# The last pair's results go to their tokens by products with a weight matrix, and the table of the other results is read and added beside them

## The reference, cut to what matters

```python
x = first_block(...)             # mixing part, then: x = x + hier_moe(rms_norm(x), ...)
h = x
h = h + mixers(rmsnorm(h)) ...   # second layer
h = h + hier_moe_2(rmsnorm(h), ...)
return rmsnorm(h, norm_final)

# either MoE, for token t with experts e1, e2 and gates g1, g2:
#   y_e(t) = (silu(x_t @ w1[e]) * (x_t @ w3[e])) @ w2[e]
#   h_t    = h_t + g1 * y_e1(t) + g2 * y_e2(t)
```

## Time and profile before

| | us |
|---|---|
| median of 3 runs (lowest, highest) | 2476.98 (2476.9, 2477.67) |
| the profiled execution's own time | 2479.46 |
| its span in the trace | 2477.7 |
| PE busy | 2146.9 (87%) |
| DVE busy | 694.2 (28%) |
| ACT busy | 351.8 (14%) |
| POOL busy | 124.4 (5%) |

### The profile page before, as it was taken

How to read it: one execution, slowest core, us unless ns; L and a number is a source line. 1 busy time by engine, 2 the same in 40 slices (tenths; PEclk the granted TensorE clock), 3 DMA queues, 4 the chain that set the end, 5 groups by cost and what they waited for, 6 DMA issues and landing times.

```text
span 2477.7 us, 26940 instructions
## 1 busy us (share of the span) xinstructions
PE 2146.9 (87%) x11637; PEld 1061.0 (43%) x11637; DVE 694.2 (28%) x1734; ACT 351.8 (14%) x675; POOL 124.4 (5%) x154
## 2 busy tenths in 40 slices
PE   7999999969878787399999999999999697787883
PEld 3455444434333333155665754445554343333331
DVE  2236561241000000213678554121022410000002
ACT  3101220110000000012222442100021100000001
POOL 4000000000000000001011100000000000000000
PEclk9999999979999989789999999999999699999996
DMA  5212112449999999721100101152332499999994
GB/s 192 92 35 88 49 42 95 178 176 422 427 427 428 426 427 428 257 85 26 28 3 2 70 1 59 61 203 97 107 136 85 148 427 427 426 428 427 426 428 178
DMA packets 92714, 524.29 MB, mean 212 GB/s; under 512 B 13013, under 2 KB 27530, under 8 KB 66986
## 3 DMA queue, kind: packets, MB, share of 16 engines
q1 hardware_dynamic: 77712, 483.43, 48.1%
q10 hardware_dynamic: 5130, 21.56, 2.3%
q0 software_dynamic: 9744, 17.47, 2.0%
HBM read 514.02 MB, written 25.17 MB: 218 GB/s over the span
## 4 chain that ended last, share of the span: by engine, by line
PE 67%; DMA 23%; DVE 6%; issue 2%; ACT 1%; ACTq 0%; DVEq 0%; POOLq 0%
PE ps L198 64%; DMA SC<-in_w 5%; DMA SC<-in_w_e_up 4%; DMA RING<-in_w_e_up 3%; DMA RING<-in_w 3%; DMA XT<-in_w_e_down 3%; DMA XT<-in_w 3%; DMA SC<-in_w_e_down 1%; DVE X L1680 1%; DMA SC<-ytab 1%; PE ps L363 1%; PE ps L1339 1%; PE ps L2629 0%; DMA ytab<-SC,ST 0%; DMA SC<-xrows,ST 0%
## 5 line engine op out<-in xcount | busy, mean ns | idle before, releaser
L198 PE MATMUL ps<-SC 64*64 64x64 f32 (+4 forms) x5872 | 700.0, 328 | 93.2 <-issue 23.5
L198 PE MATMUL ps<-RING,SC 128*64 128x512 f32 (+2 forms) x1872 | 681.3, 621 | 77.3 <-issue 48.0
L198 PE MATMUL ps<-XT,RING 128*128 128x512 f32 x1104 | 495.2, 602 | 6.1 <-DVE SC L1960 3.3
L198 PEld LDWEIGHTS ps<-SC 64*64 64x64 f32 (+2 forms) x5872 | 341.1, 146 | 329.1 <-issue 291.7
L198 PEld LDWEIGHTS ps<-RING,SC 128*64 128x64 f32 (+2 forms) x1872 | 239.6, 159 | 379.9 <-issue 379.9
L198 PEld LDWEIGHTS ps<-XT,RING 128*128 128x128 f32 x1104 | 208.3, 192 | 255.4 <-issue 248.4
L1474 DVE TENSOR_TENSOR SC<-SC,ps 128x512 f32<-128x512 f32 x32 | 22.0, 688 | 721.8 <-PE ps L198 721.8
L198 PE MATMUL ps<-XT,SC 128*64 128x512 f32 x352 | 161.4, 613 | 21.6 <-DMA SC<-in_w_e_up 10.9
L198 PE MATMUL ps<-RING,XT 128*128 128x512 f32 (+2 forms) x448 | 158.2, 506 | 0.0
L198 PE MATMUL ps<-SC,RING 128*128 128x512 f32 (+2 forms) x448 | 116.2, 426 | 0.0
L198 PEld LDWEIGHTS ps<-RING,XT 128*128 128x128 f32 x448 | 78.0, 201 | 73.6 <-issue 73.2
(11 more groups left out here) (390 smaller groups left out, 1429.1 us busy)
## 6 DMA issues: line engine op xcount, KB each, us to landing
RING<-in_w SPq DMA_DIRECT2D x43, 2048.0 KB, 33.8
SC<-in_w SPq DMA_DIRECT2D x42, 2048.0 KB, 34.1
RING<-in_w_e_gate SPq DMA_DIRECT2D x22, 2048.0 KB, 34.2
SC<-in_w_e_down SPq DMA_DIRECT2D x17, 2048.0 KB, 33.2
RING<-in_w_in SPq DMA_DIRECT2D x16, 2048.0 KB, 8.3
SC<-in_w_e_up SPq DMA_DIRECT2D x16, 2048.0 KB, 34.7
XT<-in_w SPq DMA_DIRECT2D x11, 2048.0 KB, 33.2
RING<-in_w_e_up SPq DMA_DIRECT2D x10, 2048.0 KB, 32.6
```

Of the source, the lines that this page charges most:

```text
L198: return e.matmul(out, l, r, start=st, stop=sp, skip_group_check=True)
```

## The change

In short, and in the order of the code: `ytab` is filled with zeros at the start of the kernel; three masked copies of the gates are made, `gp` for results in rows of pairs before the last, `gh` for the last pair (`LAST` = 15), `go` for overflow pairs; a 128 x 512 matrix `hot` with the gate of the last pair's rows for each token is made on DVE before the last pair's up eviction and turned on PE into `hot2` (rows of the pair by tokens); the last pair isn't scattered: eight products `hot2` (128 tokens of `tt`) times YS (512 columns) give what it adds, and DVE adds these to X out of PSUM; the reads of the table are issued by SP, ahead of `mix2_first` in `moe0`, and DVE adds the table with `gp`, three tiles of it before the first addition of the products. The norm `n2` squares all four tiles on ACT. The final norm multiplies by the gain first and by the root last, shared between DVE and ACT; the gain is loaded by SP.

```diff
     def norm_a(e, m):
-        for i in range(0, m.nt, 2):
+        for i in range(0, m.nt, m.by):                  # n2 has by=1: all four on ACT, none on DVE
...
     def set_g(e):                                       # at its end
+        W.wait_ge(*HG.on("f", 1))
+        e.memset(SC[:, 9, :], 0.0).then_inc(*S.up("g"))
+        W.wait_ge(*S.last("g"))
+        for i in range(4):
+            e.dma_start(ytab.rearrange("(p a b) n -> a p (b n)", a=4, b=2)[i], SC[:, 9, :]).then_inc(*S.up("dz", "zeros"))
...
     def df_a(e):                                        # and likewise in df_v_
+                    if n == "k":
+                        W.wait_ge(*S.on("zeros"))
...
     def s(e):                                           # in moe, after the 96 loads
-            if ahead is not None:
-                ahead(e)
+            for i in (5, 6):
+                for f in slots.put(i, ("yb", bi, i), (c, ("X", NT - 1)))[1]:
+                    W.wait_ge(*f)
+            for x in range(2):
+                W.wait_ge(*slots.on((f"m{bi}", LAST, 2, x)))
+                W.wait_ge(*c.on("y", LAST - 1 - x))
+            for tt in range(NT):
+                e.dma_start(YB[tt], ytv[tt]).then_inc(*c.up(f"dyb{tt}", "yb", tt))
+            ahead(e)
...
     def p(e):                                           # in moe
                 up_p(e, c, q, c.take, w)
                 if q + 1 < NPAIR:
                     turn_e(e, c, q + 1, c.take)
+                else:
+                    b, free = c.take("hot")
+                    W.wait_ge(*free)
+                    W.wait_ge(*c.on("hot"))
+                    for tt in range(NT):
+                        i = e.transpose(b[:, tt * 128:(tt + 1) * 128], hot[:, tt * 128:(tt + 1) * 128], ident[:, :])
+                    i.then_inc(*c.up("p", "hot T"))
                 down_p(e, c, q, c.take, w)
+            for tt in range(NT):
+                for hf in range(2):
+                    b, free = c.take("add", tt, hf)
+                    W.wait_ge(*free)
+                    W.wait_ge(*c.on("ev", "hot"))
+                    W.wait_ge(*c.on("ev", "down", LAST, hf))
+                    mm(e, b[:, :], hot2[:, tt * 128:(tt + 1) * 128], YS[:, LAST % 2, hf * 512:(hf + 1) * 512]).then_inc(*c.up("p", "add", tt, hf))
...
     def a(e):                                           # in moe; ACT evicts hot2 and, for the last pair, both halves of down
+                if q == LAST:
+                    W.wait_ge(*c.on("hot T"))
+                    e.activation(hot2, c.at("hot")[:, :], AF.Copy).then_inc(*c.up("a", "ev", "hot"))
...
-            W.wait_ge(*c.on("y", NPAIR - 1))
-            W.wait_ge(*c.on("y", NPAIR - 2))
-            for tt in range(NT):
-                e.dma_start(YB[tt], ytab.rearrange("(t p c) n -> t p (c n)", p=128, c=2)[tt]).then_inc(*c.up(f"dyb{tt}", "yb", tt))
...
     def v(e):                                           # in moe
+            hots_v(e)
+            up_v(e, c, LAST, c.at)
+            n_over = over(e)
+            for kind, tt in (("table", 0), ("table", 1), ("table", 2), ("add", 0), ("table", 3), ("add", 1), ("add", 2), ("add", 3)):
+                if kind == "table":
+                    W.wait_ge(*c.on("yb", tt))
+                    rows(e, tt, gp, c, "v")
+                else:
+                    for hf in range(2):
+                        xs = X[:, tt, hf * 512:(hf + 1) * 512]
+                        W.wait_ge(*c.on("add", tt, hf))
+                        W.wait_ge(*c.last("v"))
+                        e.tensor_tensor(xs, xs, c.at("add", tt, hf)[:, :], A.add).then_inc(*c.up("v", "ev", "add", tt, hf))
+                    c.also("v", "X", tt)
...
+            segments(e, n_over, pair_v, late)            # the branch now stands behind the additions
...
+        def rows(e, tt, g, f, s):
+            for k in range(2):
+                W.wait_ge(*f.last(s))
+                e.scalar_tensor_tensor(X[:, tt, :], YB[tt][:, k * D:(k + 1) * D], g[:, k, tt:tt + 1], X[:, tt, :], A.mult, A.add).then_inc(*f.up(s))
+        def hots_v(e):
+            W.wait_ge(*c.on("turn", LAST - 1, 1))
+            W.wait_ge(*c.last("v"))
+            for k, dst in ((0, hot), (1, hot2)):
+                for tt in range(NT):
+                    e.tensor_scalar(dst[:, tt * 128:(tt + 1) * 128], iotf[:, :], prf[:, k, tt:tt + 1], gh[:, k, tt:tt + 1], A.is_equal, A.mult).then_inc(*c.up("v"))
+            W.wait_ge(*c.last("v"))
+            e.tensor_tensor(hot, hot, hot2, A.add).then_inc(*c.up("v", "hot"))
...
     def g(e):                                           # in moe
-            scatter(e, c, NPAIR - 1, 0)
...
+    def fn_first(e):                                    # on SP, behind moe1's reads of the table
+        for f in slots.put(4, "fn", (FN, ("y", NT - 1)))[1]:
+            W.wait_ge(*f)
+        e.dma_start(fn_g, t["norm_final_2"].rearrange("(a n) -> a n", a=1).to_broadcast([128, D])).then_inc(*FN.up("dg", "g"))
...
     def fn_v(e):
+        W.wait_ge(*FN.on("g"))
+        for i in range(NT):
+            W.wait_ge(*M1.on("X", i))
+            e.tensor_tensor(fn_Y[:, i, :], X[:, i, :], fn_g, A.mult).then_inc(*FN.up("v", "xg", i))
         W.wait_ge(*FN.on("sq", NT - 1))
         mean_rsq_v(e, FN, fn_R, "nrm", fn_ss, 1.0 / D, 1e-6)
-            e.scalar_tensor_tensor(fn_Y[:, i, :], X[:, i, :], fn_R.y[:, i:i + 1], fn_g, A.mult, A.mult).then_inc(*FN.up("v", "y", i))
+        W.wait_ge(*FN.on("nrm", "rs"))
+        for i in (1, 3):                                # ACT does 0 and 2 in fn_a
+            W.wait_ge(*FN.on("xg", i))
+            e.tensor_scalar(fn_Y[:, i, :], fn_Y[:, i, :], fn_R.y[:, i:i + 1], None, A.mult).then_inc(*FN.up("v", "y", i))
```

More of the change, by code:

```diff
@@ L344, in norm_v @@
         c = m.c
-        for i in range(1, m.nt, 2):
+        for i in range(1, m.nt, 2) if m.by == 2 else ():
             for f, step in m.ready(i):
@@ L348, in norm_v @@
             e.tensor_tensor_reduce(m.xn[:, i, :], m.src[:, i, :], m.src[:, i, :], 1.0, 0.0, A.mult, A.add, m.ss[:, i:i + 1]).then_inc(*c.up("v", "sq", i))
-        for i in range(0, m.nt, 2):
+        for i in range(0, m.nt, m.by):
             W.wait_ge(*c.on("sq", i))
@@ L1243, in moe @@
         OH = st(2 * NT * 32).rearrange("p (k a b) -> p k a b", k=2, b=32)
-        v1, v2, g1, g2 = st(NT), st(NT), st(NT), st(NT)
+        v1, v2 = st(NT), st(NT)
+        G, gp, gh, go = (st(2 * NT).rearrange("p (a b) -> p a b", a=2) for _ in range(4))
+        g1, g2 = G[:, 0, :], G[:, 1, :]
         hots = [(st(NT * n).rearrange("p (a b) -> p a b", b=n), st(NT)) for n in (4, 8, 8)]
@@ L1265, in moe @@
         NPAIR = NE // 2
+        LAST = NPAIR - 1
+        hot, hot2 = XG[:, LAST % 2 ^ 1, 0:512], XG[:, LAST % 2 ^ 1, 512:1024]
+        ytv = ytab.rearrange("(t p c) n -> t p (c n)", p=128, c=2)
         RT = Flow(book, f"rt{bi}", (3, 4, 5, 6, 7))
@@ L1282, in s @@
                 slots.put(n, f"free{n}", *users)
-            slots.put(6, "free6", *((RT, ("xrows", tt)) for tt in range(NT)))
+            slots.put(6, "free6", (RT, ("xrows",)))
             for p in range(NPAIR):
@@ L1304, in load, with over, segments @@
                         e.dma_start(view(slots.views[4 + n % 3], j), WS[j][bass.ds(i_, 1)].rearrange("a (p k) n -> p (a k) n", p=128)).then_inc(*o.up(f"dw{n % 3}", "load", q, j, x))
-            segments(e, load)
+            segments(e, over(e), load)
             join(e)
-        def segments(e, body):
+        def over(e):
             W.wait_ge(*c.on("nov"))
-            v = e.value_load(nov[0:1, NOV:NOV + 1], min_val=0, max_val=NOV)
+            return e.value_load(nov[0:1, NOV:NOV + 1], min_val=0, max_val=NOV)
+        def segments(e, v, body, after=None):
             def one(q):
@@ L1321, in one @@
                         one(q + 1)
+                    if q == 0 and after is not None:
+                        after()
                     e.wait_ge(*c.on("nov"))
@@ L1413, in pair_p @@
                 down_p(e, o, q, banks, ow)
-            segments(e, pair_p)
+            segments(e, over(e), pair_p)
             join(e)
@@ L1672, in pair_v, with late @@
                 down_v(e, o, q, fixed_at)
-            segments(e, pair_v)
-            join(e)
-            for tt in range(NT):
-                W.wait_ge(*c.on("yb", tt))
-                for k, gk in ((0, g1), (1, g2)):
-                    W.wait_ge(*c.last("v"))
-                    e.scalar_tensor_tensor(X[:, tt, :], YB[tt][:, k * D:(k + 1) * D], gk[:, tt:tt + 1], X[:, tt, :], A.mult, A.add).then_inc(*c.up("v"))
-                c.also("v", "X", tt)
+            def late():
+                e.wait_ge(*o.on("yb"))
+                for tt in range(NT):
+                    rows(e, tt, go, o, "x")
+                o.also("x", "X")
+            segments(e, n_over, pair_v, late)
+            join(e)
+        def rows(e, tt, g, f, s):
[6 more added lines that the diff above has]
+            for k, dst in ((0, hot), (1, hot2)):
```

(12 more changed lines are left out.)

46 lines of the change are left out of this document (26 added, 20 removed).

## The result

The changed kernel took 2463.99 us (median of 4 runs, 2458.94 to 2464.41) against 2477.32 for the kernel before beside it (4 runs, 2476.90 to 2479.44). The ratio is 0.994, with a 95% interval of 0.9923 to 0.9957, so it is faster by 13.3 us. The forecast was 2463.6. The profiled execution went from 2479.46 to 2464.04 and its span from 2477.7 to 2462.3, 15.4 us less.

The account below looks back on a forecast made before the run. Each MoE was taken as bound by its weight loads, which the change leaves alone; only serial end pieces of 39 and 36 us could be won. -14.5 + 1.1 = -13.4 us, median 2476.98 to 2463.6, range 2460 to 2468.

Parts of the forecast that it names:

- When the reads start: Table reads issue at 1012.1 in the first MoE, 16 us earlier; at 2441.85 in the second, held by slot 5.
- DVE's run: Table and product additions on DVE at both MoE ends take 16.6 us, against 10.7 before, with no wait inside.
- The four reads come in faster than this: At both ends, table reads land faster than DVE's 1.34 us per operation, so DVE sets the pace.
- A DVE wait on a product: Sign against the forecast: DVE waiting for PE's products; these were expected in time, lateness taken as 0.
- The first end: End of the first MoE: earlier reads, less the longer DVE run, gain 14.5 us, bounds 11.5 to 15.5.
- From there on the work is as before: After the root starts at 1034.9 in the first end's norm, nothing changes, so the first lx product comes at 1044.9.
- The cover of the loads: mix2 loads move behind the table reads; wl lands at 1033 with 12 us of cover, so cost 0.
- The rival that it comes late: After the first MoE, wl completes at 1048.3, 3.4 us after PE wants it: 2467.0 us; chance 9%.
- The second end: End of the second MoE and final norm: loss 1.1 us, bounds -0.5 to 2.5; last tile 1.65 us later.
- The branch: On DVE between the second end's last addition and the gain products: costs 0.4 us, at most 1.8.
- The zeros: Table zeros written from about 40 us end by 52, cost 0; rival that they delay k's eviction: 2525, chance 4%.
- both ends gain: Rival: without slot 5 as last wait, second-end reads start at 2432.0, DVE ends 9.9 us earlier: 2453.7; chance 4%.

Follow-up runs that it names:

- the kernel with slot 2: Changed kernel, but in the second MoE the table's upper half is read into slot 2 instead of slot 5: 2453.52 us, ratio 0.991.
- the kernels that have one end each: Changed kernel with the old path put back in the other MoE and its norm: first end alone 2460.40 us, second end alone 2478.26 us.
- the kernel with the first end alone: Changed kernel with the second MoE and final norm put back as before: 2460.40 us, ratio 0.9935.
- the second trace of the changed kernel: The changed kernel run once more with no edit: 2461.58 us, ratio 0.994 to the kernel before.
- the kernel with the loads first: Changed kernel, but in the first MoE SP issues the next layer's 11 loads ahead of the table reads: 2483.31 us, ratio 1.0027.

## Why the prediction was right

**When the reads start: right at both ends.** Predicted 1012.1, measured 1012.47, by the landing of the last down weights (1012.31), as the kernel without that wait shows: there they go out at 1002.22. They were to go out about 1 us before the last down products begin; the reads went out 2.4 to 2.6 us before them in five traces and 0.1 us behind their start in three, since those products follow PE's work before them and not the reads. At the second end they go out at 2424.68, the moment in which ACT begins to evict the last down products. That the slot, not the reads' other conditions, holds them there was the central step, and the kernel with slot 2 shows it.

**DVE's run: the way right, its length short.** Predicted 16.6 us, with 16 to 17 and no wait inside as the sign. At the first end it was 17.1 (1017.37 to 1034.44), at the second 17.9 (2429.53 to 2447.44), of which 0.95 is a wait for the second read, and there the sign failed. "The four reads come in faster than this" did not hold: the second read landed 8.0 us after its issue (2425.05), 0.95 us after DVE wanted it. What the prediction left out is the load of the final gain, which SP issues 0.65 us behind the last read (2426.65). Where that load follows the reads, the second read took 7.6 to 8.4 us, in all eleven such traces; in the traces in which nothing or a load of `mix2` follows, and no weights are ahead, it took 6.8 to 7.1, also at the first end of the same executions and at the old second end (7.0 and 6.8). At that pace it would have landed as DVE wanted it. No run moves the gain's load alone, so this is read from the traces and not shown by an edit.

A DVE wait on a product, a sign that would have been against me, came at the first end with this order of adding only when the reads went out 10 us earlier.

**The first end: 14.5 predicted, and 0.5 and 1.4 us were missing behind it.** The root began at 1035.76 (predicted 1034.9). In absolute time L came at 1047.57 instead of 1044.9. Three things make up the 2.7 us. The root was 0.9 late: 0.37 by the reads' issue and 0.5 by DVE's run. The first two small operations of the root took 0.38 and 0.45 us where such operations took 0.17 elsewhere, 0.5 us in all; the runs do not settle why. And from the first transpose to L it took 8.04 instead of 6.65 us, 1.4 more. (Over the traces it is 7.9 to 8.1 with this first end, and 6.65 and 7.17 with the old one, so 0.7 to 1.5.) "From there on the work is as before" is the step that failed. The windows say why. Before, PE's clock rose during the transposes (us; busy PE, PEld, DVE, ACT, POOL; PEclk; DMA share; GB/s):

```profile
1052.70:1055.00 2.30, 1.97 (x8) 1.47 (x9) 0.55 (x1) 1.73 (x3) 0.00 (x0) 0.50 0.00 0
1055.00:1059.30 4.30, 3.49 (x26) 3.25 (x24) 3.02 (x6) 2.33 (x4) 0.00 (x0) 0.86 0.07 29
```

After, it stayed near the 1.2 GHz level through nearly all of them, though PE had idled for 10.5 us and not for 32.6:

```profile
1034.00:1039.50 5.50, 0.00 (x0) 0.01 (x1) 3.76 (x15) 2.06 (x4) 2.04 (x5) 0.50 1.19 295
1039.50:1047.00 7.50, 6.86 (x32) 6.12 (x32) 3.07 (x5) 4.06 (x6) 0.00 (x0) 0.57 0.99 304
```

I had asked for the clock only in the eight products, where nothing was lost, and not in the transposes.

The gain of this end, measured against D, was 13.62 in the profiled pair, and 14.45 between the kernels that have one end each (47.24 - 32.79). The +1.81 before D is a difference between executions: in the kernel with the first end alone D is at 1012.83. The 14.45 takes a D that lies 2.4 us behind the reads' issue; by the second trace of the changed kernel the same subtraction gives 11.2 (46.31 - 35.14). The 13.5 between the means of L depends on no such choice. 1.1 us of the gain came from squaring all tiles on ACT: from DVE's last addition to the root it was 2.42 us before (1047.02 to 1049.44) and is 1.32 now. No run has that edit alone.

**The cover of the loads: right.** Of the matrix `wl` the third and the last piece landed at 1030.7 and 1031.5 (forecast 1033), 16 us before L. The rival that it comes late is refuted, and PE waited for no weight. What the loads would cost in another place of the queue, the kernel with the loads first shows: all of the gain.

**The second end: loss 1.1 predicted, 1.8 to 2.4 measured.** The last tile of X was ready 22.76 us after the down products' end (2447.44 - 2424.68) where 4.85 + 16.6 = 21.45 had been forecast. Before it was 19.9, so the last tile came 2.9 us later, where 1 to 2 had been the sign. The 1.3 us are the 0.95 of the wait and, for the rest, DVE's run. The branch was forecast at 0.4 and cost nothing: L3067 begins at 2447.40, on the heels of the last addition. The Trainium skill's page "Runtime: NRT & Kernel Launch", section "Instruction fetch mechanics", says that a taken branch out of the current two pages stalls the engine for a fetch. No stall shows at this place; whether the target lies in these pages no row tells. The norm went as forecast: four products 4.63 us (forecast 4.87), and 6.93 us from the first store (2455.37) to the end of the span (forecast 6.9). The "some 400 GB/s" beside that figure is a slip, since 2.1 MB in 6.9 us are 304 GB/s; and the fourth read before was issued at 2447.37 and not at 2447.7, so it landed 12.3 us after the first issue and not 12.6. Neither changes the sum.

**The zeros: right,** no cost shows. The rival "both ends gain" gave 2453.7; the full change refutes it, and the kernel that removes its obstacle reaches 2453.52. T to end fell by 8.9 us there where the rival had 9.9, so the agreement to 0.2 us is in part chance.

**The sum.** -13.4 was forecast and the medians gave -13.3 beside the first runs and -14.5 beside the second. The agreement to 0.4 us in the first is luck in part: D to L and T to end give -11.8 in the profiled pair, -12.4 between the kernels with one end each (-14.45 + 2.06, both with a D 2.5 us behind the landing of the last weights), and the 13.5 between the means of L less 1.8 to 2.4 gives 11.1 to 11.7. The gain of the first end fell short and the loss of the second was larger than forecast, and the clock of the untouched mixer moves an execution by up to 5 us, part of which lies in the profiled pair's 15.4.

## What to carry to other kernels

Moving work off a chain pays only where its inputs can really come earlier: look up which slot their buffer takes over and who still reads it, before counting overlap. Splitting an addition into two kinds lengthens the serial run (17 us for 10.7 here), so it wins with an early start, loses without one, and then should do first the part whose data are there first. Place the transfer on the critical path ahead of the prefetches in its queue. And before stretches of two traces are compared, look whether the mark they start from is what the change waits for.

## What the runs showed of the hardware

How long PE had idled before the norm's 32 transposes did not by itself set how long they took, and the longest idling had the shortest transposes: behind 8.1 and 8.3 us of idling 6.7 and 6.6 us, behind 10.4 to 13.0 us 7.0 to 7.2 us (eight traces), and behind 32 to 33 us 5.8 to 6.3 us (three traces). In the changed kernel (10.5 us) the clock over them was 0.57, in the kernel before (32.6 us) 0.50 and then 0.86. Filling 8.2 us ahead of them with useless transposes brought the 32 real ones from 7.15 to 3.66 us.

Four stores of 2.1 MB together took 6.9 to 7.0 us from the first issue to the end of the span in all fourteen traces, with their issues spread over 3.85 us or crowded into 2.88; only an earlier first store moved the end.

Of four reads of 1 MB issued within 1.8 to 2.2 us, with nothing else ahead of them, the second landed 6.8 to 7.1 us after its issue, and 7.6 to 8.4 us where a load of 0.5 MB, one row copied to all 128 partitions, was issued 0.65 to 0.8 us behind the fourth. Whether that load is the cause no run shows by itself.
